# Hybrid decoder layer on one core: the delta rule's triangular inverse in 32-column blocks, and a reordered last expert

## The chip, the cores and the metric

One core of a Trainium2 chip runs the whole program. The metric is device time in microseconds; lower is better. The engines are TensorE (PE; its weight loads are shown as PEld), VectorE (DVE), ScalarE (ACT), GpSimd (POOL) and SyncE (SP, here only a queue of DMAs). TensorE runs at one of two clock levels, 2.4 GHz (shown as 1.0) or 1.2 GHz (shown as 0.5).

## The reference

One decoder layer over 1024 tokens of width 1024, all in float32: an RMS norm; one input projection; a gated MLP mixer (4 heads of 128) beside a gated DeltaNet mixer (4 heads of 128); an output projection with residual; an RMS norm; a router that takes 4 of 32 experts; the experts (width 1024, clamped SwiGLU); a residual; a final RMS norm. What the change touches is the DeltaNet's triangular solve and the end of the layer:

```python
lower = jnp.where(tril_strict, jnp.einsum('bhnid,bhnjd->bhnij', kb, kc) * decay, 0.0)
a_mat = lower + jnp.eye(c, dtype=lower.dtype)
rhs = jnp.concatenate([vc * bc[..., None], kb * jnp.exp(gc)[..., None]], axis=-1)
sol = lax.linalg.triangular_solve(a_mat, rhs, left_side=True, lower=True, unit_diagonal=True)
...
return ((up + 1.0) * (gate * jax.nn.sigmoid(SWIGLU_ALPHA * gate))) @ w_down[e] + b_down[e]
...
return rmsnorm(h, final_norm_g)
```

## The kernel before

Three stages follow each other: projections (to about 361 us), mixers (to about 690 us), experts (to the end). Each engine has its own program, and semaphores tie them; the order of the work is the order in which each engine's program is written.

**Mixers.** The 1024 tokens are 8 chunks of 128, handled as 4 pairs i = 0 to 3; within a pair the two chunks s = 0 and 1 go through each step one behind the other, four heads side by side, so that most tiles are 128 x 512 (four heads of 128 x 128). PSUM has 8 banks; chunk s has banks 4s to 4s+3. For each chunk the kernel needs the inverse T of the unit lower triangular 128 x 128 matrix of each head, and it uses its transpose U.

The inverse is built by doubling (`chunk(i)` on PE and DVE). Level 0 is done elementwise: T starts as the identity minus the 2 x 2 off-diagonal entries (`first_t` on POOL, L891, then two DVE operations, L1310 and L1312), and U as its transpose (`first_u` on POOL, L862 and L864). LT, the masked and scaled product of keys and keys, is made by DVE at L1308. Then for levels l = 1 to 6, for each s: PE multiplies LT by T (`four`, L1036; for l = 5 and 6 only the blocks that count, `lower_blocks`, L1044); DVE masks the product with the level's mask into P (L1321, L1324, L1328); PE multiplies U by P (L1036, L1044); DVE subtracts the result from T (L1338, L1344). From l = 2 on PE also transposes T (L1128) and ACT copies it out of PSUM as the new U (L990). Level 6 is applied to U instead (L1145, L1349). A float32 product leaves two MATMUL records and two LDWEIGHTS records in the trace, a transpose one.

Between the levels stands work of the pair before: two sets of 8 transposes (`h_columns`, L1063, at l = 1 and 3) and the router's logits of both chunks (L1069, at l = 5). After level 6 PE makes W (`four`, L1036), then values, state and outputs. Ahead of level 1 PE makes keys times keys (L1085), keys times queries (L1091), and transposes values (L1104) and keys (L1112). DVE also makes AT (L1316) and ke (L1334) in this stretch. POOL masks the decays E (L845), scales the queries (L850), and writes the token lists by indirect DMA (L883). After the inverse and the state, DVE and ACT already make the decays of the next pair (`start`).

**Last expert.** An expert's `gate_up` on PE (L1787) makes 8 slices m; for each, DVE clamps (`clamps`, L1957 to L1961), ACT applies the sigmoid (L1697), and POOL multiplies twice (`gated`, L1622 and L1625), which frees DVE for slice m + 2. `down_rows` (L1800) takes slice k of hT as soon as it is there. In the last expert the final norm is mixed in: SP has begun to load the 8 tiles of h back (L1559); ACT's `early_squares` takes two tiles' squares (L1702) behind each of the sigmoids m = 4 to 7; DVE takes the means, POOL the roots, DVE scales tiles (L2003), and SP stores them (L1563). The last expert's own 128 rows are treated apart: when its `gated` is over, POOL gathers those rows of h (`hg`, L1656); DVE adds the bias (L2040) and the expert's result (L2030), ACT squares (L1733), and POOL scatters them to the output (L1663) once all tiles are stored.

Of the kernel before, what the change touches and what calls it, by code (L numbers as in the profile page):

```python
# [20 lines left out]
KT, TT = D // P, SEQ // P  # L21
# [22 lines left out]
PARTS, HB = 5, 64  # L44

C_ID, C_TRI, C_ONE, C_M0T, C_LV = 0, 128, 256, 384, 512
C_IOTA = C_LV + LEVELS * 128
# [5 lines left out]
NCST = C_PART + 1  # L53


def program(nc, x, norm_mix_g, w_in, gm_norm_g, gm_ws, gm_bs, dn_conv_w, dn_a_log, dn_dt_bias,
# [6 lines left out]
    with ctx:  # L63
# [14 lines left out]
        m0t = cst[:, C_M0T:C_M0T + 128]  # L78
# [4 lines left out]
        def level(l):  # L83
            return cst[:, C_LV + 128 * l:C_LV + 128 * (l + 1)]
# [29 lines left out]
        AW = 46784  # L114
# [61 lines left out]
        ixf, rkf = [[cut(4) for _ in range(2)] for _ in range(2)]  # L176

# [36 lines left out]
        def heads(ap):  # L214
            return ap.rearrange("p (h c) -> p h c", h=H)

# [623 lines left out]
        def _(pool):  # L840
# [17 lines left out]
            def first_u(i):  # L858

                for s in range(2):  # L860
                    pool.wait_ge(S("LT", s), i + 1)
                    v.tensor_tensor(heads(Um[s]), heads(LT[s]), over_heads(m0t), ALU.mult).then_inc(S("U0a", s), 1)  # L862
                    pool.wait_ge(S("U0a", s), i + 1)
                    v.tensor_tensor(heads(Um[s]), over_heads(ident), heads(Um[s]), ALU.subtract).then_inc(S("U0", s), 1)  # L864
# [21 lines left out]
            def first_t(i):  # L886

                for s in range(2):
                    if i:
                        pool.wait_ge(S("TU", s), 5 * i)  # L890
                    v.tensor_tensor(heads(Tm[s]), over_heads(level(0)), over_cols(sub_all[:, 2 * i + s, :]), ALU.mult  # L891
                                    ).then_inc(S("T0", s), 1)

            first_t(0)
            for s in range(2):
                masked(0, s)
            for i in range(PAIRS):
                first_u(i)
# [7 lines left out]
                if i + 1 < PAIRS:  # L906
                    first_t(i + 1)
                    start(i + 1)
# [20 lines left out]
        def _(act):  # L929
# [40 lines left out]
            def finish(i):  # L970
# [16 lines left out]
                for l in range(2, LEVELS):  # L987
                    for s in range(2):
                        act.wait_ge(S("TU", s), 5 * i + l - 1)
                        a.activation(Um[s], bank(4 * s), ACT.Copy).then_inc(S("Uc", s), 1)  # L990
                    if i and l in (2, 4):
                        hT_copy(i - 1, l // 2 - 1)
                    if i and l in (3, 5):
                        h_norm(i - 1, l // 2 - 1)
                    if i and l == 6:
                        for s in range(2):
                            logits(i - 1, s)
# [31 lines left out]
        def _(pe):  # L1029
# [9 lines left out]
            def lower_blocks(out_bank, left, right, l, name):  # L1039
                b = 1 << l  # L1040
                for h in range(H):
                    for z in range(0, P, 2 * b):
                        lo, hi = slice(h * P + z, h * P + z + b), slice(h * P + z + b, h * P + z + 2 * b)
                        last = t_.matmul(out_bank[z + b:z + 2 * b, lo], left[:, hi], right[:, lo], start=True, stop=True)  # L1044
# [32 lines left out]
            def chunk(i):  # L1077
# [9 lines left out]

                def queries(s):
# [8 lines left out]
                for s in range(2):  # L1097
                    queries(s)
                for s in range(2):
                    b0, c = 4 * s, 2 * i + s  # L1100
                    if i:
                        pe.wait_ge(S("Eb", s), i + 1)
# [12 lines left out]
                for l in range(1, LEVELS):  # L1115
                    for s in range(2):
                        b0 = 4 * s
                        pe.wait_ge(S("Tl", s), 6 * i + l)
                        if l < PARTS:
                            four(bank(b0 + 2), LT[s], Tm[s], S("LTp", s))  # L1120
                        else:
                            lower_blocks(bank(b0 + 2), LT[s], Tm[s], l, S("LTp", s))
                        if l == 2:
# [1007 lines left out]
```

## Time and profile before

| | us |
|---|---|
| median of 3 runs | 2282.27 (2279.67 to 2283.38) |
| profiled execution, device time | 2280.05 |
| its span | 2278.3 |
| PE busy | 2214.6 (97%) |
| DVE, ACT, POOL busy | 747.3, 372.1, 586.4 |

The profile is of one execution; its span is what the engines show and its device time is 1.75 us longer. PE busy counts the time in which at least one matmul record is open, and ends of matmuls are modelled, so it does not tell PE at its peak. Times below are counted from the start of the span.

### The profile page before, as it was taken

Reading aid. Unit: us, or ns where it says so; the run is one execution under the profiler, and the core shown is the slowest. Engines: PE = TensorE matmul, PEld = TensorE weight load, DVE = VectorE, ACT = ScalarE, POOL = GpSimd, SP = SyncE. Lnnn points to the kernel's source line nnn. Section 1 sums busy time; section 2 is a strip of 40 time slices with the busy share of each in tenths; the row PEclk is TensorE's granted clock in tenths of the full one; section 3 lists DMA queues with packets and bytes.
Section 4 is the critical chain, followed back from the end, with each engine's and each line's share of the span. In section 5 each row is a group of like instructions: output and inputs, shape, how many; then the busy total and the mean of one; then the engine's idle time right before and its main releaser. Section 6 shows DMA issues by size and latency. Waiting matters only on the chain.

```text
span 2278.3 us, 45334 instructions
## 1 busy us (share of the span) xinstructions
PE 2214.6 (97%) x18872; PEld 1832.8 (80%) x18873; DVE 747.3 (33%) x1759; ACT 372.1 (16%) x845; POOL 586.4 (26%) x808
## 2 busy tenths in 40 slices
PE   8999998999996999999999999999999999999997
PEld 5665446678765989898898989889898898898975
DVE  2234777454632172222222222222222222213223
ACT  2222653223220101010100101001010010110102
POOL 1133222322423122222222223222232223222312
PEclk9999999999997999999999999999999999999999
DMA  8000113011017788888989799998999979899897
GB/s 266 1 0 19 21 36 154 19 47 47 29 38 252 265 266 279 289 268 275 297 273 319 237 337 296 293 322 284 306 302 293 334 243 336 272 349 351 261 322 285
DMA packets 381977, 505.81 MB, mean 222 GB/s; under 512 B 19248, under 2 KB 295284, under 8 KB 381720
## 3 DMA queue, kind: packets, MB, share of 16 engines
q1 hardware_dynamic: 362632, 459.58, 60.3%
q0 software_dynamic: 19136, 43.29, 7.1%
q8 instruction: 151, 2.47, 0.5%
q14 instruction: 58, 0.48, 0.1%
HBM read 472.19 MB, written 33.05 MB: 222 GB/s over the span
## 4 chain that ended last, share of the span: by engine, by line
PE 73%; SPq 5%; issue 2%; DVE 2%; DMA 1%; POOL 1%; ACT 0%; DVEq 0%; ACTq 0%; POOLq 0%
PE ps L1787 37%; PE ps L1815 12%; PE ps L1800 8%; PE ps L1213 5%; PE ps L1036 3%; SPq L784 3%; PE ps L1765 2%; SPq L1545 1%; PE ps L1774 1%; PE ps L1128 1%; DMA arena<-h_dram,arena 1%; PE ps L1069 1%; SPq L1555 1%; DMA arena<-h_dram 1%; PE ps L1044 0%
## 5 line engine op out<-in xcount | busy, mean ns | idle before, releaser
L1787 PEld LDWEIGHTS ps<-arena 128*64 128x64 f32 (+1 forms) x12544 | 961.6, 152 | 20.0 <-issue 17.7
L1787 PE MATMUL ps<-arena 128*64 128x108 f32 (+29 forms) x12544 | 973.9, 273 | 2.5 <-issue 1.7
L1957 DVE TENSOR_SCALAR arena<-ps,arena 128x108 f32<-128x108 f32 (+29 forms) x256 | 92.3, 361 | 1062.4 <-PE ps L1787 1058.4
L1622 POOL TENSOR_TENSOR arena<-arena 128x108 f32<-128x108 f32 (+29 forms) x256 | 133.1, 520 | 1076.0 <-DVEq L1964 1076.0
L1815 PE MATMUL ps<-arena 128*128 128x224 f32 (+14 forms) x1920 | 273.4, 303 | 0.2 <-POOL arena L1625 0.2
L1697 ACT ACTIVATE arena<-arena 128x108 f32<-128x108 f32 (+29 forms) x256 | 81.5, 318 | 1172.5 <-DVE arena L1957 1172.5
L1815 PEld LDWEIGHTS ps<-arena 128*128 128x128 f32 x1920 | 270.4, 189 | 1.0 <-POOL arena L1625 0.4
L1800 PE MATMUL ps<-arena 128*128 128x512 f32 x544 | 238.6, 596 | 2.7 <-POOL arena L1625 2.7
L1800 PEld LDWEIGHTS ps<-arena 128*128 128x128 f32 x544 | 102.5, 191 | 126.7 <-issue 121.6
L536 PE MATMUL ps<-arena 128*128 128x384 f32 (+1 forms) x512 | 171.5, 494 | 2.1 <-DVE arena L639 2.1
L536 PEld LDWEIGHTS ps<-arena 128*128 128x128 f32 x512 | 97.4, 193 | 68.2 <-issue 2.6
L549 PE MATMUL ps<-arena 128*128 128x512 f32 x336 | 146.3, 593 | 0.8 <-DVE arena L686 0.8
L549 PEld LDWEIGHTS ps<-arena 128*128 128x128 f32 x336 | 63.6, 190 | 80.4 <-issue 78.4
L1625 POOL TENSOR_TENSOR arena<-arena 128x108 f32<-128x108 f32 (+29 forms) x256 | 123.0, 480 | 20.1
L1213 PE MATMUL ps<-arena 128*128 128x512 f32 x256 | 112.9, 595 | 0.8 <-DVE arena L1381 0.8
L232 POOL TENSOR_TENSOR small<-small,cst 128x4 f32<-128x4 f32 (+1 forms) x35 | 27.7, 795 | 332.7 <-DVE small L229 323.2
L1213 PEld LDWEIGHTS ps<-arena 128*128 128x128 f32 x256 | 47.5, 190 | 56.1 <-issue 54.5
L1958 DVE TENSOR_SCALAR arena<-ps,arena 128x108 f32<-128x108 f32 (+29 forms) x256 | 89.9, 351 | 0.0
L1613 POOL DMA_INDIRECT h_dram<-arena x46 | 80.6, 1752 | 30.7 <-issue 15.8
L1036 PE MATMUL ps<-arena 128*128 128x128 f32 x640 | 83.2, 280 | 3.8 <-DVE arena L1321 2.9
L1717 ACT ACTIVATE arena<-ps,arena 128x224 f32<-128x224 f32 (+14 forms) x120 | 47.9, 399 | 231.8 <-PE ps L1815 231.8
L1036 PEld LDWEIGHTS ps<-arena 128*128 128x128 f32 x640 | 76.8, 191 | 5.7 <-issue 3.6
(275 smaller groups left out, 1591.0 us busy)
## 6 DMA issues: line engine op xcount, KB each, us to landing
arena<-in_exp_w_gu SPq DMA_DIRECT2D x256, 1024.0 KB, 10.4
arena<-in_exp_w_down SPq DMA_DIRECT2D x64, 2048.0 KB, 11.6
arena<-in_exp_b_down SPq DMA_DIRECT2D x17, 512.0 KB, 10.1
arena<-in_x SPq DMA_DIRECT2D x16, 512.0 KB, 8.9
arena<-in_w_in SPq DMA_DIRECT2D x8, 1024.0 KB, 9.6
h_dram<-arena SPq DMA_DIRECT2D x16, 512.0 KB, 2.8
arena<-in_w_out SPq DMA_DIRECT2D x1, 4096.0 KB, 14.2
arena<-h_dram SPq DMA_DIRECT2D x8, 512.0 KB, 13.5
```

What stands on the lines that cost most here:

```text
L536: last = t_.matmul(bank(bk)[:, to:to + width], yT[:, k, t * P:(t + 1) * P], wuvz[:, k, c0:c0 + width], start=(k == 0), stop=(k == KT - 1))
L549: last = t_.matmul(to, left[:, k, :], right[:, k, :], start=(k == 0), stop=(k == KH - 1))
L1036: last = t_.matmul(out_bank[:, c], left[:, c], right[:, c], start=start, stop=stop)
L1213: last = t_.matmul(bank(4 * s + 1 + n), mixT[s][:, k, :], wout[:, k, 512 * n:512 * (n + 1)], start=(k == 0), stop=(k == KT - 1))
L1622: v.tensor_tensor(gmn[m % 2][:, 0:n], gmn[m % 2][:, 0:n], umn[m % 2][:, 0:n], ALU.mult).then_inc(S("gum", m % 2), 1)
L1625: v.tensor_tensor(hT[:, m, 0:n], gmn[m % 2][:, 0:n], sg[m % 2][:, 0:n], ALU.mult).then_inc(S("hT"), 1)
L1697: a.activation(sg[m % 2][:, 0:n], gmn[m % 2][:, 0:n], ACT.Sigmoid, scale=ALPHA).then_inc(S("sg", m % 2), 1)
L1787: last = t_.matmul(bank(m % 4)[c0:c1, q * CAP:q * CAP + n], wslot[g][:, k, 256 * q + c + c0:256 * q + c + c1], xT[:, k, 0:n], start=(k == ...
L1800: last = t_.matmul(bank(6 + q), hT[:, k, 0:P], wslot[4 + q][:, k, :], start=(k == 0), stop=(k == KT - 1))
L1815: last = t_.matmul(bank(6 + d % 2)[:, 0:n], wslot[g][:, k, c:c + P], hT[:, k, 0:n], start=(k == 0), stop=(k == KT - 1))
L1957: v.tensor_scalar(gmn[r][:, 0:n], bank(m % 4)[:, 0:n], of[:, m:m + 1], LIMIT, ALU.add, ALU.min).then_inc(S("gmn", r), 1)
L1958: v.tensor_scalar(umn[r][:, 0:n], bank(m % 4)[:, CAP:CAP + n], of[:, 8 + m:9 + m], LIMIT, ALU.add, ALU.min)
```

## The change

- The levels l = 1 to 4 of the inverse stay inside the 32 x 32 blocks on the diagonal. They are held compactly: Tc and Uc are 128 x 128 for a chunk (4 heads of 32 columns; the four blocks of a head lie in the four quarters of the partitions). PE makes the compact keys product itself (`key_blocks`), DVE makes the level 0 T and transposes it blockwise (`v.transpose`).
- `diag_blocks` replaces `four`: 16 products with a weight tile of 32 columns and 32 moving columns each, whose outputs lie in the four quarters of PSUM's partitions. The U side is summed in PSUM: an identity product adds the old U, the second product adds the level's term (the masks are now negative). DVE transposes the result into the new Tc, ACT copies it as Uc. PE's transposes (L1128) go away.
- Level 5 joins 32 blocks to 64 (`join_blocks`, `joined_upper`), with a compact LT copied by ACT (LH) and an expanded U built by DVE; level 6 works as before with a compact T (Th) and copies instead of subtracting.
- LD, the decays masked to the diagonal blocks, is made ahead by POOL (`diag_decays`), which loses `first_u`; DVE multiplies both LD and LT with the keys product. P is still a 128 x 512 tile, written by DVE from a 128 x 128 PSUM tile by a broadcast over the four blocks, for l = 1 to 5.
- Last expert: all 8 sigmoids come first, then ACT squares tiles 2 to 7; DVE squares tiles 0 and 1 itself after the clamps; POOL's two roots come after the gather of `hg`; DVE scales tiles 0 to 3, adds the bias to `hg`, scales tiles 4 to 7, and then does the two halves of the last rows.

```diff
+            def diag_blocks(out_bank, left, right, name=None, start=True, stop=True):
                 for h in range(H):
+                    for z in range(Z):
+                        q = slice(QB * z, QB * (z + 1))
+                        last = t_.matmul(out_bank[q, QB * h:QB * (h + 1)], left(h, z), right[:, QB * h:QB * (h + 1)],
+                                         start=start and h == 0, stop=stop and h == H - 1)
...
+            def joined_upper(out_bank, left, right, name):
+                for h in range(H):
+                    for z, c in ((0, 0), (1, 0), (2, 2)):
...
                 for s in range(2):
+                    if i:
+                        pe.wait_ge(S("Eb", s), i + 1)
+                    key_blocks(s)
...
+                        if l < LEVELS - 2:
+                            diag_blocks(bank(b0 + 2), block_columns(LD[s]), Tc[s], S("LTp", s))
+                        elif l == LEVELS - 2:
+                            pe.wait_ge(S("LH", s), i + 1)
+                            join_blocks(bank(b0 + 2), LH[s], Tc[s], S("LTp", s))
...
+                        if l < LEVELS - 2:
+                            diag_blocks(bank(b0 + 3), block_ident, Uc[s], stop=False)
+                        pe.wait_ge(S("Pl", s), 6 * i + l)
+                        if l < LEVELS - 2:
+                            diag_blocks(bank(b0 + 3), block_columns(Pm[s]), Uc[s], S("TP", s), start=False)
+                        elif l == LEVELS - 2:
+                            joined_upper(bank(b0 + 3), Pm[s], Uc[s], S("TP", s))
...
# DVE, chunk(i)
+                    v.tensor_tensor(Tc[s], Tc[s], bank(4 * s + 3)[:, 0:P], ALU.mult).then_inc(S("Gc_used", s), 1)
...
+                    v.tensor_tensor(blocks(Tc[s]), blocks(Tc[s]), over_heads(ident_b), ALU.add)
...
+                    v.transpose(Uc[s], Tc[s]).then_inc(S("Tl", s), 1)
...
+                    v.tensor_tensor(LD[s], LD[s], bank(4 * s + 2), ALU.mult)
+                    v.tensor_tensor(LT[s], LT[s], bank(4 * s + 2), ALU.mult)
...
+                        if l < LEVELS - 1:
+                            v.tensor_tensor(Pm[s].rearrange("p (h z c) -> p h z c", h=H, z=Z),
+                                            blocks(bank(4 * s + 2)[:, 0:P]).unsqueeze(2).broadcast_to([P, H, Z, QB]),
+                                            blocks(level(l)).unsqueeze(1).broadcast_to([P, H, Z, QB]), ALU.mult).then_inc(S("Pl", s), 1)
...
-                            v.tensor_tensor(Tm[s], Tm[s], bank(b0 + 3), ALU.subtract).then_inc(S("Tl", s), 1)
+                            v.transpose(Tc[s], bank(b0 + 3)[:, 0:P]).then_inc(S("Tl", s), 1)
...
# ACT, last expert
-                sigmoid(r, ROWS[r], early_squares if r == LAST else lambda m: None)
+                sigmoid(r, ROWS[r])
+                if r == LAST:
+                    for t in range(2, TT):
+                        tile_square(t, 0)
...
# DVE, last expert
-            for t in range(2, 4):
+            for t in range(2):
+                dve.wait_ge(S("hc_in", t), 16)
+                v.tensor_tensor_reduce(yt[:, t, :], hc[:, t, :], hc[:, t, :], 1.0, 0.0, ALU.mult, ALU.add, small[:, 32 + t:33 + t])
```

## Rows read from the trace of the kernel before

**Rows 1.** The page: busy time by engine, and the chain that ended last.

```profile
PE 2214.6 (97%) x18872; PEld 1832.8 (80%) x18873; DVE 747.3 (33%) x1759; ACT 372.1 (16%) x845; POOL 586.4 (26%) x808
...
PE 73%; SPq 5%; issue 2%; DVE 2%; DMA 1%; POOL 1%; ACT 0%; DVEq 0%; ACTq 0%; POOLq 0%
```

**Rows 2.** Busy by stretch: length, PE, PEld, DVE, ACT, POOL, clock, DMA, GB/s.

```profile
375.32:389.33 14.01, 14.01 (x122) 13.77 (x122) 8.84 (x14) 3.58 (x6) 1.19 (x1) 1.00 0.56 230
389.33:396.14 6.81, 6.42 (x113) 5.17 (x112) 3.99 (x12) 2.39 (x4) 0.00 (x0) 1.00 0.01 2
438.88:450.14 11.26, 10.42 (x89) 9.98 (x88) 10.59 (x15) 5.38 (x18) 5.71 (x4) 1.00 0.12 49
450.14:464.72 14.58, 14.58 (x130) 14.44 (x129) 8.02 (x14) 6.58 (x11) 1.09 (x2) 1.00 0.09 37
464.72:475.22 10.50, 10.11 (x146) 8.82 (x145) 3.98 (x12) 3.78 (x7) 0.00 (x0) 1.00 0.42 151
...
626.13:638.11 11.98, 11.59 (x146) 10.00 (x145) 3.98 (x12) 3.78 (x7) 0.00 (x0) 0.86 0.38 133
```

**Rows 3.** Timeline, level 2 of pair 2: start, length, engine, line, records, [idle before].

```profile
530.12 1.06 PE L1036 MATMUL ps<-arena 128*128 128x128 f32 x8
...
531.01 0.60 PE L1128 MATMUL ps<-cst,arena 128*128 128x128 f32 x4
531.21 0.69 DVE L1321 TENSOR_TENSOR arena<-ps,cst 128x512 f32<-128x512 f32 x1 [0.65 <-PE ps L1036]
...
532.78 3.00 PE L1036 MATMUL ps<-arena 128*128 128x128 f32 x24
```

**Rows 4.** Timeline, matmuls with weight tiles under 128 columns.

```profile
544.70 0.45 PE L1044 MATMUL ps<-arena 128*32 128x32 f32 x16
...
471.46 0.68 PE L1044 MATMUL ps<-arena 128*64 128x64 f32 x8
...
790.21 7.04 PE L1787 MATMUL ps<-arena 128*64 128x88 f32 x179
```

**Rows 5.** Timeline at the start of pair 2, and DVE by form over its inverse.

```profile
519.79 1.16 PE L1085 MATMUL ps<-arena 128*128 128x128 f32 x8
...
525.37 1.27 DVE L1316 TENSOR_TENSOR arena<-arena,ps 128x512 f32<-128x512 f32 x2
...
L1324 DVE TENSOR_TENSOR arena<-ps,cst 128x128 f32<-128x128 f32 x4 | 1.0, 284 | 0.3 <-PE ps L1044 0.3
```

**Rows 6.** The router's logits of pair 1 (timeline), and the stretch behind them.

```profile
547.75 3.90 PE L1069 MATMUL ps<-rw,arena 128*128 128x32 f32 x32
...
551.20:554.60 3.40, 3.40 (x23) 2.89 (x22) 0.42 (x1) 0.60 (x1) 0.00 (x0) 0.50 0.78 283
```

**Rows 7.** Timeline of the last two experts, and the stores by line.

```profile
2206.49 13.90 PE L1800 MATMUL ps<-arena 128*128 128x512 f32 x32
...
2220.32 27.74 PE L1787 MATMUL ps<-arena 128*64 128x126 f32 x512
...
2245.54 1.06 ACT L1702 ACTIVATE arena<-arena 128x1024 f32<-128x1024 f32 x1 [7.07 <-DMA arena<-h_dram]
...
2248.05 0.31 ACT L1697 ACTIVATE arena<-arena 128x126 f32<-128x126 f32 x1
...
2257.25 9.69 PE L1800 MATMUL ps<-arena 128*128 128x512 f32 x18 [1.98 <-POOL arena L1625]
2257.48 1.97 POOL L1656 DMA_INDIRECT arena<-h_dram,arena  x1 [0.28 <-issue]
...
2260.96 4.87 DVE L2003 SCALAR_TENSOR_TENSOR arena<-arena,small,fin_g 128x1024 f32<-128x1024 f32 x4 [1.17 <-POOL small L232]
...
2267.17 1.28 DVE L2040 SCALAR_TENSOR_TENSOR arena<-arena 128x1024 f32<-128x1024 f32 x1 [1.33 <-DMA arena<-h_dram,arena]
...
2273.84 1.06 POOL L1663 DMA_INDIRECT out<-arena  x1 [1.71 <-DVE arena L2051]
...
out<-arena SPq DMA_DIRECT2D x8, 512.0 KB, 5.1
```

More of the change, by code:

```diff
@@ L884, in lists @@
                                             ids[:, t, j, :], None).then_inc(S("listed"), 16)
[L886 to L894, printed above, removed]
+            for s in range(2):
+                first_T(0, s)
+            for s in range(2):
+                diag_decays(0, s)
             for s in range(2):
                 masked(0, s)
+            for s in range(2):
+                v.memset(LH[s], 0.0)
+                v.memset(Th[s], 0.0)
+            pool.drain()
+            pool.sem_inc(S("zeros"), 1)
             for i in range(PAIRS):
-                first_u(i)
                 if i:
@@ L906, in _ @@
                 if i + 1 < PAIRS:
-                    first_t(i + 1)
+                    for s in range(2):
+                        first_T(i + 1, s)
+                    for s in (1, 0):
+                        diag_decays(i + 1, s)
                     start(i + 1)
@@ L1086, in keys, with key_blocks @@
                     last.then_inc(S("Gk", s), 1)
+                def key_blocks(s):
+                    for h in range(H):
+                        k_ = qkvT[:, 4 + h, cols(2 * i + s)]
+                        for z in range(Z):
+                            q = slice(QB * z, QB * (z + 1))
+                            last = t_.matmul(bank(4 * s + 3)[q, QB * h:QB * (h + 1)], k_[:, q], k_[:, q], start=True, stop=True)
+                    last.then_inc(S("Gc", s), 1)
                 def queries(s):
@@ L1097, in chunk @@
                 for s in range(2):
+                    if i:
+                        pe.wait_ge(S("Eb", s), i + 1)
+                    key_blocks(s)
+                for s in range(2):
                     queries(s)
@@ L1657, in _ @@
                                     ).then_inc(S("hg_in"), 16)
-            tile_roots(1, 0)
+            for q in range(2):
+                tile_roots(q, 0)
             pool.wait_ge(S("l_var"), 1)
@@ L2041, in _ @@
             dve.drain()
+            for t in range(4, TT):
+                tile_scale(t, 0)
             for q in range(2):
                 last_half(q)
+            dve.wait_ge(S("hT"), 8 * NE)
             dve.wait_ge(S("last_h"), 2)
```

207 lines of the change are left out of this document (122 added, 85 removed).

## The prediction

> **What bounds the kernel now.** I read the page first: PE is open 97% of the span and carries 73% of the chain that ended last [rows 1]. Work taken off another engine is then worth nothing, except where PE waits for it. Next the busy times by stretch, to see what the inverse costs [rows 2]. In pair 1 the stretch from the keys product to level 2 is 11.26 us, levels 2 to 4 are 14.58, level 5, the router's logits and level 6 are 10.50: 36.3 together. Pair 0, without the logits, has 14.01 and 6.81 for the last two, and pair 3 11.98 for the last, at a mean clock of 0.86. The four inverses are thus some 145 us, and in levels 2 to 4 PE is open in every moment (14.58 of 14.58): there the time is PE's own work.
>
> The timeline of one level shows its make-up [rows 3]. A `four` is 8 records in 1.06 us; the last record is open 0.28, so PE gives it (1.06 - 0.28) / 7 = 0.112 per record, 0.90 in all. A set of transposes is 4 records, 0.44. A level has four `four` and two sets of transposes: 3.58 + 0.88 = 4.5 us, and from 530.12 to 534.57 (16 records into the run of 24 that begins at 532.78) it took 4.45. DVE's masking (0.69) and subtraction lie beside it.
>
> **The new level, step by step.** Each level from 1 to 4 now issues, per chunk, three `diag_blocks` (LD times T, the identity times U, P times U) of 16 products, 32 records each: 192 records for both chunks instead of 40. So all hangs on the time of one such record, r. No row has four column groups; the nearest have one or two [rows 4]. 16 records with 32-column weights, in two column groups, took 0.45 us: (0.45 - 0.20) / 15 = 17 ns per record, which is 34 ns within a group. 64-column weights with 64 moving columns in one group took (0.68 - 0.22) / 7 = 65 ns. The experts' 64-column weights in two groups, with 88 moving columns, took (7.04 - 0.24) / 178 = 38 ns, less than the 65: two groups run side by side at no visible loss. If four do, r = 34 / 4 = 8.5 ns; if no more than two do, or if the pace of issue is what the 17 shows, r = 17. I take 12: doubling the groups from one to two is shown, from two to four is not, and the result depends little on where r lies below 13, as the next lines show.
>
> With r = 12 a `diag_blocks` is 0.385 us. From the moment that T of chunk 0 is there: first product to 0.385 (its last record closes at 0.57), DVE's masking 0.60 to 1.29 and for chunk 1 to 1.87 (two in 1.27, as L1316 in [rows 5]), meanwhile PE does chunk 1's product and the identity product (to 1.16), then P times U from 1.35 to 1.74, and chunk 1's two to 2.50. DVE's blockwise transpose of a 128 x 128 tile is not in the trace; the nearest row is a 128 x 128 operation from PSUM, 0.284 [rows 5]; bounds 0.2 and 0.69 (a full 512 wide one). It ends at about 2.25, under chunk 1's product, so PE never waits for it. ACT's copy of U is under the next level's first products. A level: 2.5 us. With r = 8.5 DVE and the semaphores bound it, 2.2; with r = 17 PE is full again, 6 x 0.54 = 3.25. `h_columns` adds its 0.90 at level 3, of which a PE with gaps hides a third.
>
> Levels 2 to 4 of a pair: 3 x 2.5 + 0.6 = 8.1 against 14.6, so -6.5 (r = 8.5: -7.3; r = 17: 10.65, -4.0). Pair 0 has no `h_columns`: 7.5 against 14.0, -6.5.
>
> **Start of a pair.** This is where the change gives back. Two `key_blocks` of 32 records each come in PE's order (0.8 us), and DVE gets more to do before level 1 can begin: for both chunks a 128-wide product, addition and transpose (6 x 0.28), two LD products at 0.64 more than before, less the two T products and additions (2 x 0.68, 2 x 1.23 to 1.65) of today. Set out from 519.79 [rows 5]: DVE cannot start before the compact keys are there (1.5), has Tc and Uc at 3.4, LD and LT of both chunks at 6.1, AT (which stands before the level's masks in DVE's queue) at 7.4, then the masks of level 1 to 8.7; PE's last product of level 1 ends near 9.6, `h_columns` near 10.5. Today level 2 begins at 530.12, 10.3 later. So +0.3 (r = 8.5: -0.2; r = 17: +0.9). If POOL's LD were late it would add to this; POOL needs it right after the decays, some 20 us ahead of its use, and it gives up `first_u`. Only in pair 0 is there no such lead, and the clock is low there: +1.
>
> **Levels 5 and 6.** Level 5 has 16 and 24 records per chunk and two full-width masks; PE reaches the logits at 2.1 to 2.3 instead of 3.05: -0.8. The new work of ACT and DVE for it (U expanded, LH, Th) lies under the 3.9 us of logits [rows 6]; in pair 0 it lies bare and takes the gain back. Level 6 loses two sets of transposes and the wait for U's copy: 2.45 against 3.76, -1.3.
>
> **Sum for the mixers** at r = 12: pairs 1 to 3: -6.5 + 0.3 - 0.8 - 1.3 = -8.3 each; pair 0: -6.5 + 1 - 0.9 = -6.4; together -31.3. At r = 8.5 -36, at r = 17 3 x -5.2 - 3.9 = -19.5.
>
> **The clock.** In pair 2 it fell to 1.2 GHz during the logits, whose records move only 32 columns each, and stayed there for the next 3.4 us [rows 6]; pair 3's last stretch has 11.98 where pair 1's has 10.50 at full clock [rows 2], so a fall costs 1.5 us, and two of three pairs pay it. The new levels 1 to 5 also move 32 columns per record, and DVE leaves PE gaps in them. I charge one fall more per pair, 4 us in all (bounds: 0, and the rival below).
>
> **The last expert.** ACT sat idle 7.07 us for the first tile of h, so that the sixth sigmoid came at 2248.05, when PE was at the end of `gate_up` (2220.32 + 27.74) [rows 7]. So `down_rows`, 13.9 us when undisturbed, ended only at 2266.94, and POOL's gather of the last rows, behind `gated`, was issued at 2257.48, landed at 2267.17 and set the end. With the sigmoids first, hT is complete at about 2250.5, PE ends at 2262, and the gather is issued at 2250.5, landing even at 9.7 us by 2260.2. What is late next is DVE: two squares (1.3 each, as L2003) to 2252.5, four scales from 2253.7 to 2258.8, the bias to 2260.1, four scales (4.87) to 2265.2, two halves to 2266.7. Today they cannot end before 2267.17 + 1.28 + 2 x 0.69 = 2269.8; the rest of the chain is the same, unless the last store, 5.1 us to landing from 2265.3, comes last: 2270.4 against today's issue of the scatter at 2273.84. Gain 3 us, bounds 1.5 (stores slower) and 4.
>
> **Forecast.** -31.3 + 4 - 3 = -30. The sum is made against the profiled execution, 2280.05 (span 2278.3), which lies 2.2 below the median shown: 2250 there, 2253 against a median of 2282.3 with 1 us left for what I priced too well. Its own range, r from 8.5 to 14 and the clock's charge from 0 to 8: 2242 to 2259.
>
> **Rivals.**
> - A, two groups' pace: r = 17. For it: the only row with 32-column weights shows it, and each record also needs a weight load. Against: 34 ns within a group fits loads that run beside each other. Time: -19.5 + 3 - 3 = -19.5, 2263.
> - B, a long burst of 96 or 192 small records is issued more slowly than the burst of 16 that the row shows: r = 25, midway between 17 and the 34 of one group by itself. A level is then 192 x 25 = 4.8 us on PE against 4.5, the start +1.9, levels 5 and 6 -1.9: +0.6 per pair, +2 in all, tail -3, clock +2: 2283, no change. Against it: the experts' 179 records run as evenly as short ones [rows 4].
> - C, slower: the clock falls in level 1, as it did in the logits, and stays at 1.2 GHz to level 6, and r doubles from 17 to 34. A level is then 6 x 1.09 = 6.5, three of them and `h_columns` +6, the start +4, level 6 -1.3: +8 to +9 per pair, +33; tail -3: 2312. The place is every pair's levels 1 to 5; it decides from r = 24 on, where the pair is even. For it: [rows 6]. Against: today's level 6 ran cold for 3.4 us only and then came back, though its records are small too.
> - D, the change doesn't reach the end of the tail: the stores' bandwidth, not ACT, sets it. Then only the 3 us go: 2256, inside the forecast.
>
> On B, the Trainium skill (TensorEngine Tiling, section Instruction Overhead) says that each matmul has about 60 cycles of overhead, so that a few moving columns take as long as 60; by that rule the result would be B's. As far as bursts of 16 go, this case's trace disagrees: 17 ns per record, weight load included.
>
> **Chances.** Forecast (with D) 0.60, A 0.23, B 0.07, C 0.07, better than the range 0.03. Faster by over 0.2% (4.6 us, about what can be told from no change) 0.87, within 0.06, slower 0.07. The range that holds 8 in 10 reaches from all groups in parallel to A with a little more clock loss: 2242 to 2267.
>
> **What would show it.** The level's spacing of L1321's successor: 2.5 us (2.2 and 3.25 the bounds, 4.8 for B, 6.5 for C). Records of a `diag_blocks`: 32 in 0.27 to 0.54 us plus the last one's length. The clock in levels 1 to 5: 1.0 in most of it. Level 2 of pair 2 begins 10.5 us after the second keys product. DVE's transpose near 0.28; if it were 0.69, a level is 2.9. At the end: PE done near 2262 less the mixers' gain, no idle in it. The prediction is wrong if r is over 17, if the clock falls inside the levels for more than a third of them, or if a level is bound by an ACT or DVE operation priced here as hidden.

## The result: slower by 0.8%, and the profile after

The changed kernel took 2299.95 us (median of 4 runs, 2296.42 to 2303.46) against 2281.68 for the kernel before (4 runs, 2279.67 to 2283.38): a ratio of 1.0078, 95% interval 1.0066 to 1.009. The forecast was 2253, its range 2242 to 2267. The direction was wrong. One execution further down stands apart, 4624.37 us for the 100-record version at its second measurement; why is not known, and it is in no time and no ratio given here.

The page of the kernel after, lines that answer to [rows 1], with the queue that carries instructions:

```profile
PE 2197.6 (95%) x21592; PEld 1815.1 (79%) x21593; DVE 738.9 (32%) x1771; ACT 369.5 (16%) x881; POOL 569.8 (25%) x804
...
q8 instruction: 172, 2.82, 0.5%
...
PE 75%; issue 4%; DVE 3%; POOL 1%; DVEq 1%; DMA 1%; another core or an unknown queue 0%; POOLq 0%; ACT 0%; SPq 0%; ACTq 0%
```

PE is open 17 us less than before, in a span that is 23.3 longer (2301.6 against 2278.3): the work went down as meant, and time in which PE does nothing took its place. "Issue", time in which an engine waits for nothing that the profile shows, went from 2% to 4% of the chain. The mean granted clock went from 0.988 to 0.969. The queue q8 moved 151 packets before and 172 now: 21 more, for 5520 more instructions on the page (50854 against 45334), which is one packet for 263.

Where the 23.3 lie: the program reaches the first keys product 1.7 later (in the profiles of the later runs this point lies between 362.1 and 364.3 us, so that is spread between executions); from there to W, the four pairs together took 165.4 instead of 145.5 (+19.9); behind W, pairs 1 and 2 take 1.4 longer each (0.78 of it one more wait for DVE ahead of the products in L1138); from the last W to the experts nothing changed; first product of the experts to the end of the span, 1.3 less, the tail in it. The busy rows by stretch, pair 0 from the last products of level 1 to the first joins of level 5, then pair 1 in three stretches as in [rows 2], and the last stretch of pair 3:

```profile
376.45:400.00 23.55, 11.66 (x702) 10.54 (x704) 8.33 (x18) 2.63 (x10) 0.00 (x0) 0.55 0.38 153
448.90:460.06 11.16, 9.74 (x313) 8.93 (x311) 8.73 (x19) 6.65 (x23) 0.00 (x0) 1.00 0.13 51
460.06:475.59 15.53, 9.60 (x585) 8.73 (x584) 5.63 (x14) 4.61 (x11) 1.08 (x2) 0.67 0.10 38
475.59:490.69 15.10, 12.80 (x164) 12.28 (x149) 4.78 (x10) 4.33 (x13) 0.00 (x0) 0.58 0.31 106
648.74:662.72 13.98, 12.97 (x161) 12.35 (x149) 4.81 (x10) 4.07 (x12) 0.00 (x0) 0.51 0.32 115
```

The start of pair 1 takes 11.16 against 11.26. Levels 2 to 4 take 15.53 against 14.58 (8.1 were forecast), though PE is open only 9.60 of it and DVE 5.63: no engine's work fills this stretch. Level 5, logits and level 6 take 15.10 against 10.50, at a clock of 0.58.

The timeline of pair 2 shows why, PE's rows of levels 2 to 4 and of the logits (start, length, records, [idle before <- what ended it]):

```profile
544.80 0.46 PE L1084 MATMUL ps<-arena 128*32 128x32 f32 x32 [1.20 <-DVE arena L1415]
...
550.04 0.35 PE L1084 MATMUL ps<-arena 128*32 128x32 f32 x18 [0.72 <-issue]
...
553.77 0.48 PE L1084 MATMUL ps<-arena 128*32 128x32 f32 x18 [2.07 <-issue]
554.01 0.67 PE L1084 MATMUL ps<-arena,cst 128*32 128x32 f32 x32
...
557.78 0.48 PE L1084 MATMUL ps<-arena 128*32 128x32 f32 x18 [2.08 <-issue]
558.20 1.97 PE L1127 MATMUL ps<-cst,arena 128*128 128x128 f32 x8
...
566.05 6.42 PE L1133 MATMUL ps<-rw,arena 128*128 128x32 f32 x32
```

The record itself is as fast as the best bound: 32 records in 0.46, the last of them open 0.20, so (0.46 - 0.20) / 31 = 8.4 ns. But after 128 records (550.04 to 553.77, then to 557.78) PE stops, with every input there, and goes on 2.1 us later. 256 records took 7.74 us, 30 ns each. From 554 on the row of 32 records takes 0.67 instead of 0.46: the clock has fallen to 1.2 GHz. Read in steps of 1 us, the granted clock of pair 2 is 0.50 from 554 to 563, 1.00 from 564 to 566, and 0.50 again from 567 to 577, through the rest of the logits (6.42 against 3.90 in [rows 6]) and level 6. Pairs 1 and 3 also fall twice: in the levels (464 to 474, 638 to 645) and from level 5 on (478 to 491, 649 to 662).

### The profile page after: what moved, and what is told of

It reads as the page before. It is cut to its first block, busy times and chain, and to the rows that moved or that the text cites. A ratio compares the mean times of both kernels' runs of the same rounds, so it can differ in the third digit from the quotient of the medians.

```text
span 2301.6 us, 50854 instructions
## 1 busy us (share of the span) xinstructions
PE 2197.6 (95%) x21592; PEld 1815.1 (79%) x21593; DVE 738.9 (32%) x1771; ACT 369.5 (16%) x881; POOL 569.8 (25%) x804
## 3 DMA queue, kind: packets, MB, share of 16 engines
q8 instruction: 172, 2.82, 0.5%
## 4 chain that ended last, share of the span: by engine, by line
PE 75%; issue 4%; DVE 3%; POOL 1%; DVEq 1%; DMA 1%; another core or an unknown queue 0%; POOLq 0%; ACT 0%; SPq 0%; ACTq 0%
PE ps L1878 39%; PE ps L1906 12%; PE ps L1891 10%; PE ps L1297 4%; PE ps L1856 2%; PE ps L1084 2%; PE ps L1865 1%; PE ps L1133 1%; PE ps L1077 1%; PE ps L1149 0%; PE ps L1127 0%; POOL arena L1717 0%; PE ps L1255 0%; POOL arena L1714 0%; DMA arena<-h_dram,arena 0%
## 5 line engine op out<-in xcount | busy, mean ns | idle before, releaser
L1906 PEld LDWEIGHTS ps<-arena 128*128 128x128 f32 x1920 | 270.4, 189 | 1.0 <-POOL arena L1717 0.4
L1891 PEld LDWEIGHTS ps<-arena 128*128 128x128 f32 x544 | 102.0, 190 | 122.1 <-issue 121.4
L551 PEld LDWEIGHTS ps<-arena 128*128 128x128 f32 x512 | 97.9, 194 | 68.7 <-issue 3.5
L1717 POOL TENSOR_TENSOR arena<-arena 128x108 f32<-128x108 f32 (+29 forms) x256 | 123.0, 481 | 20.1
L564 PEld LDWEIGHTS ps<-arena 128*128 128x128 f32 x336 | 63.6, 190 | 80.4 <-issue 78.4
L1297 PEld LDWEIGHTS ps<-arena 128*128 128x128 f32 x256 | 47.5, 190 | 56.1 <-issue 54.5
L2052 DVE TENSOR_SCALAR arena<-arena 128x108 f32<-128x108 f32 (+29 forms) x256 | 61.0, 238 | 31.6 <-issue 0.9
L734 DVE SCALAR_TENSOR_TENSOR arena<-arena,vT 128x512 f32<-128x512 f32 x72 | 66.5, 923 | 6.3 <-issue 0.9
```

Of the source, the lines that this page charges most:

```text
L551: last = t_.matmul(bank(bk)[:, to:to + width], yT[:, k, t * P:(t + 1) * P], wuvz[:, k, c0:c0 + width], start=(k == 0), stop=(k == KT - 1))
L564: last = t_.matmul(to, left[:, k, :], right[:, k, :], start=(k == 0), stop=(k == KH - 1))
L1297: last = t_.matmul(bank(4 * s + 1 + n), mixT[s][:, k, :], wout[:, k, 512 * n:512 * (n + 1)], start=(k == 0), stop=(k == KT - 1))
L1717: v.tensor_tensor(hT[:, m, 0:n], gmn[m % 2][:, 0:n], sg[m % 2][:, 0:n], ALU.mult).then_inc(S("hT"), 1)
L1891: last = t_.matmul(bank(6 + q), hT[:, k, 0:P], wslot[4 + q][:, k, :], start=(k == 0), stop=(k == KT - 1))
L1906: last = t_.matmul(bank(6 + d % 2)[:, 0:n], wslot[g][:, k, c:c + P], hT[:, k, 0:n], start=(k == 0), stop=(k == KT - 1))
```

## Experiments

All ran against the kernel before, on the same chip as the others of their group. Three theories stood against each other. **S**: instructions reach PE at a limited pace, and 192 records a level ask for more. **K**: the fallen clock is what costs. **W**: waits between PE, DVE and ACT bound the new levels. S and K can hold together.

### The tail alone

The kernel before with only the second half of the change: the last expert's sigmoids ahead of the norm's squares.

```
- gated(r, ROWS[r], (lambda m: scatter_main(r - 1, m)) if r < LAST else (lambda m: tile_roots(0, 0) if m == 5 else None))
+ gated(r, ROWS[r], lambda m: scatter_main(r - 1, m))
...
- sigmoid(r, ROWS[r], early_squares if r == LAST else lambda m: None)
+ sigmoid(r, ROWS[r])
+ if r == LAST:
+     for t in range(2, TT):
+         tile_square(t, 0)
```

> The kernel before with the new order of the last expert alone (squares after the sigmoids, two of them on DVE, roots after the gather). In the two profiles the stretch from the first record of the last down_rows to the end of the span is 30.3 us before (2247.99 to 2278.3) and 27.95 after (2273.65 to 2301.6). So 2.3 us faster than before, ratio 0.9990. If the order does nothing by itself, and the 2.3 us come from another state of the DMAs after the slower mixers: 0 us.

Measured: 2279.63 (11 runs), ratio 0.9994, interval 0.9985 to 1.0003. That is 1.9 us less, which the timing can't tell from nothing. The profiled executions say more: from the first record of the last `down_rows` to the end of the span it takes 28.0 here, as in the changed kernel (28.0), against 30.3 before. So the 2.3 us belong to the new order and not to the slower mixers ahead of it. The loss is all in the inverse.

### One identity product in place of sixteen

```
- diag_blocks(bank(b0 + 3), block_ident, Uc[s], stop=False)
+ t_.matmul(bank(b0 + 3)[:, 0:P], ident, Uc[s], start=True, stop=False)
```

The identity product of a chunk and level is now one matmul (2 records in place of 32), with the same result: 132 records a level in place of 192.

> The changed kernel, but the identity product of a level is one 128 x 128 product per chunk (2 records) in place of 16 small ones (32 records): 132 records per level instead of 192, the PE time of them about the same (0.22 us against 0.27 at full clock). Theory S (supply): PE gets its instructions at a pace of 128 records (with their weight loads) per 3.6 to 4.0 us once a stock is used up, so 60 records fewer are 1.8 us less per level, 16 levels: 25 to 29 us faster than the changed kernel, near 2273 us, and the gaps that the trace puts down to issue shrink by a third or more. Theory K (clock): the granted clock is the cause and the gaps are only its effect: PE's work is unchanged, so the time stays within 5 us of the changed kernel (2300). Theory W (the chain over DVE, ACT and semaphores bounds a level): unchanged too, 2300.

Measured: 2268.69 (6 runs, 2262.5 to 2274.28), ratio 0.9945, interval 0.993 to 0.996: 31 us less than the change, and faster than the kernel before. S had asked for 25 to 29 less; K and W had asked for no change, and both failed. PE's groups in the mixers, first of the kernel after, then of this one (records | busy, mean ns | idle before, and what ended it):

```profile
L1084 PE MATMUL ps<-arena 128*32 128x32 f32 x2048 | 34.7, 218 | 20.3 <-issue 12.3 <-DVE arena L1415 5.3 <-DVEq L1405 2.1
...
L1084 PE MATMUL ps<-arena,cst 128*32 128x32 f32 x1024 | 20.7, 219 | 17.3 <-issue 17.3
```

```profile
L1084 PE MATMUL ps<-arena 128*32 128x32 f32 x2048 | 31.6, 208 | 13.8 <-issue 5.5 <-DVE arena L1415 4.3 <-DVEq L1405 2.6
L1216 PE MATMUL ps<-arena,cst 128*128 128x128 f32 x64 | 17.7, 360 | 1.2 <-issue 1.2
```

In these groups the idle time that ends with "issue" went from 12.3 + 17.3 = 29.6 to 5.5 + 1.2 = 6.7. The waits for DVE hardly moved, 7.4 to 6.9: W explains none of the difference. Over the four pairs PE's idle time went from 42.9 to 19.4, and its open time from 122.5 to 114.1 at a mean clock of 0.981 over the span instead of 0.969. So some 24 of the 32 us that the pairs got shorter are supply; the other 8 are less open time, at a higher clock.

### The pace of supply by itself

Bursts of independent small products before the mixers, in the kernel before (ident times the table of constants, its output not used; one run, 2452.08 us, for their durations alone), and one more in the expert stage. Sixteen wide products ahead of each burst let instructions pile up.

```
+ wide(16); burst(256, 32, 32, 4)     # weights 32 wide, 32 columns moved, 4 column groups
+ wide(16); burst(256, 64, 64, 2)
+ wide(16); burst(256, 32, 128, 4)
+ wide(16); burst(256, 32, 32, 1)
```

> The kernel before with products added that nothing waits for and nobody reads, at the head of the mixers (after the load of w_out) and once behind the sixth expert: bursts of 512 records between stretches of 16 wide products (128 x 512) that keep the clock up. Burst 1: 32-column weights, 32 moving columns, four column groups. Burst 2: 64, 64, two groups. Burst 3: 32-column weights, 128 moving, four groups. Burst 4: as 1 but all in one group. In the expert stage burst 1 again, under weight traffic. S: burst 1 runs at 8.5 ns per record for one stock and then in portions of 128 records per 3.6 to 4.0 us, 12 to 15 us in all with gaps of 2 us or more, at full clock and with no wait in the program; bursts 2 and 3 (27 to 32 ns per record by width) lie at the edge, 14 to 17 us, gaps under 1 us; burst 4 (34 ns) has none, 17.4 us. If gaps belong to waits or to the low clock and not to supply: burst 1 takes 512 x 8.5 ns = 4.4 us without a gap. Under traffic: S leaves open whether the portions come later; 3.6 us if the traffic does not matter.

PE's rows of the first burst (512 records, between two wide products), and what the DMAs moved from 390 to 404 us, in 40 slices of 0.35 us:

```profile
391.83 1.48 PE L1225 MATMUL ps<-cst 128*32 128x32 f32 x150
395.33 1.30 PE L1225 MATMUL ps<-cst 128*32 128x32 f32 x128 [2.02 <-issue]
398.80 1.94 PE L1225 MATMUL ps<-cst 128*32 128x32 f32 x128 [2.16 <-issue]
402.26 1.70 PE L1225 MATMUL ps<-cst 128*32 128x32 f32 x106 [1.52 <-issue]
...
GB/s 0 0 0 0 0 0 0 0 47 0 0 0 0 0 0 0 0 0 47 0 0 0 0 0 0 0 0 0 47 0 0 0 0 0 0 0 0 0 47 0
...
q8 instruction: 4, 0.07, 1.8%
```

This is S with nothing else in it: no data is waited for, and at full speed PE takes 150 records in 1.48 us, then gets portions of exactly 128 every 3.47 us. The whole burst takes 12.1 us, where S had asked for 12 to 15. In its second gap, at 397.3, the granted clock falls from 1.00 to 0.50; the portions behind it run cold (1.94 and 1.70) and come no later, so the pace does not hang on that clock.

A record stands for two instructions, the weight load and the product, so a portion is 256 instructions, 27 ns per record. The instruction queue moved four packets in 14 us here, and nothing else was moved; on the page it has packets of 16.4 KB (2.82 MB / 172), which is 64 bytes for each of 256 instructions. The trace also shows what the 3.47 us are made of. The packets start at 392.89, 396.37 and 399.88, each 2.4 us ahead of a portion, and each 1.0 to 1.1 us after the portion before it began (the first, after the burst began). So no packet starts before PE has begun on the portion before. That is the order in the trace; what imposes it is not shown.

The other bursts had no such gaps, and their records are slower than that: 29.6 ns (64-wide weights), 28 (128 columns moved), 32 (one column group). In the expert stage, under weight traffic, the stock was 162 records and the portions came 3.47 us apart as well, after a first gap of 3.26.

### Weights of 64 columns: no gaps, but the clock

```
-                    for z in range(Z):
-                        q = slice(QB * z, QB * (z + 1))
+                    for z in range(2):
+                        q = slice(HB * z, HB * (z + 1))
```

(on top of the single identity product; the blocks off the diagonal are zero, so two 64-wide products do the work of four, and a level has 68 records.)

> As the one before, and the block products use weight tiles of 64 columns (two 32-blocks at once, the masks keep them apart), so 8 products instead of 16: 68 records per level. S: 68 records are supplied in about 2.0 us, so supply no longer binds; PE needs 64 x 0.033 + 0.45 = 2.6 us per level at full clock, level near 2.8 us, against 4.5 of before and about 4.3 to 5 of the changed kernel: 15 to 25 us faster than before, 2257 to 2267 us; no gaps put down to issue in levels 1 to 4. K: PE's share rises, the clock may hold, but if the clock was the cause the gaps stay. W: 2300, as the chain over DVE and ACT is the same.

Measured: 2286.5 (12 runs, spread from 2266.19 to 2291.56), ratio 1.0001, interval 0.9981 to 1.0021. No PE row in the levels ends its idle time with "issue" any more, so S alone would have made this the best version (2257 to 2267); two of the 12 runs come near it. Keys product to W of pairs 1 and 2, the same instructions in the same execution:

```profile
442.21:485.30 43.09, 41.80 (x546) 37.96 (x544) 19.40 (x42) 15.70 (x46) 1.08 (x2) 0.63 0.18 63
530.87:562.11 31.24, 29.76 (x546) 26.92 (x544) 19.14 (x42) 15.71 (x46) 1.09 (x2) 0.95 0.25 87
```

At a mean clock of 0.95 the pair takes 31.2, at 0.63 it takes 43.1. The clock alone is worth 12 us a pair when the work is PE's own, and the runs follow it: the two at 2266 and 2268 us have a mean clock over the span of 0.98, the eight from 2284 on 0.969 to 0.972. In the first of these two pairs the clock falls at 453 and stays at 0.50 until 487, though PE is open in every moment from 452 to 473. So it can fall and stay low without gaps for want of instructions.

### Filling PE with idle products

Two idle products per chunk and level 1 to 4, into columns of U's bank that nobody reads, in the changed kernel, in the version with 64-wide weights, and one product in the version with a single identity product:

```
+                        if l < LEVELS - 2:
+                            for _ in range(2):
+                                t_.matmul(bank(b0 + 3)[:, P:4 * P], ident, cst[:, 0:3 * P],
+                                          start=True, stop=True)
```

> The changed kernel with two idle wide products of 384 columns (ident by the table of constants, into columns 128 to 511 of U's bank, which nobody reads) per chunk at each of levels 1 to 4, behind the wait for Uc and ahead of the identity products. Nothing else changes: the 192 small records of a level stay. Price of one, from L1220 of the probe (0.44 us for 512 columns at full clock): 0.33 us, so 1.3 us of PE a level, 5.2 us a pair, 21 us in all if none of it lies in time in which PE stands idle. Theory S+K (the small records arrive at 128 per 3.5 to 4.0 us, and the clock falls because PE does little in that time): the filling lies in the idle 2 us per 128 records and costs 0 to 7 us; the granted clock stays up through the levels of more pairs, and the 10 to 12 us that a pair at 1.2 GHz loses come back for one to three pairs: 2265 to 2292 us, mean clock at 0.975 or above. Theory S alone (the supply is all of it, the clock an effect that costs nothing of its own): 2300 to 2307 us. Theory W (the chain over DVE and ACT bounds the levels): filling ahead of the identity products delays it: 2305 to 2321 us.

Measured for the changed kernel with filling: 2301.18 (5 runs), ratio 1.0086, interval 1.0073 to 1.01, mean clock 0.984. By its letter the expectation of S alone was met and that of S and K missed. But the price in it was wrong. The filling's rows in level 2 of pair 1, and the windows of that pair in the three stretches:

```profile
462.43 1.56 PE L1217 MATMUL ps<-cst 128*128 128x384 f32 x4
463.92 0.46 PE L1084 MATMUL ps<-arena,cst 128*32 128x32 f32 x32
...
464.61 1.56 PE L1217 MATMUL ps<-cst 128*128 128x384 f32 x4
```

```profile
448.83:461.74 12.91, 12.69 (x322) 10.28 (x320) 9.01 (x21) 6.92 (x24) 0.49 (x1) 1.00 0.12 44
461.74:478.35 16.61, 16.44 (x609) 10.86 (x609) 5.44 (x11) 4.71 (x10) 0.60 (x2) 1.00 0.10 37
478.35:487.87 9.52, 8.94 (x162) 8.47 (x148) 4.75 (x10) 4.07 (x12) 0.00 (x0) 0.82 0.48 167
```

A product is two records. The row shows 4 records, two products, in 1.49 (462.43 to 463.92): 0.37 a record, 0.75 a product, and I had priced a product at the time of one record. The filling is thus 64 products x 0.75 = 48 us of PE work, not 21, and it cost 1 to 2 us against the changed kernel (2301.18 and 2299.95; ratios 1.0086 and 1.0078). The four pairs took 162.7 instead of 165.4 with the 48 in them, so some 50 us of room were found. About 33 of it was idle time of PE (42.9 to 10.3 in the pairs; the "issue" groups fell from 29.6 to 3.9). The other 18 came back in PE's own work (122.5 before, 152.4 - 48 = 104 now), at a clock that is 1.00 in the levels where it was 0.67. So the third stretch of pair 1 takes 9.52 where the changed kernel had 15.10, and the levels are full of PE work that is not wanted. Of the four pairs' 163 only 115 are work that is wanted, and waits.

> The kernel with weights of 64 columns (68 records a level, no idle time for want of instructions, but pairs that run at 1.2 GHz) with the same two idle products of 384 columns per chunk and level. It adds up to 21 us of PE work and takes none away. Theory K (what this version loses is the clock alone, 12 us for each pair that falls): the clock is granted through the levels, mean 0.98 or above, and the time is 2262 to 2284 us, below the 2286.5 of the version without the filling although it does more. If the clock is not what costs: 2287 to 2308 us, mean clock as before.

Measured for 64-wide weights with filling: 2296.71 (5 runs), ratio 1.0076, interval 1.0062 to 1.009, mean clock 0.988: the clock held in all four pairs (0.92 to 1.00), and of 48 us added 10 show in the medians, 17 in the ratios (the version without filling spreads over 25). By its time K was missed again, for the same wrong price; its clock came. The other 31 to 38 came back from the clock. PE's waits gave next to nothing: in the two profiles its idle time in the pairs is 7.1 without the filling and 5.4 with it.

> The version with one identity product (132 records a level, 2268.7 us, mean clock 0.979 to 0.983) with one idle product of 384 columns per chunk and level (0.33 us each, 10.5 us in all if none lies in idle time). Theory S+K: about half lies in the idle time that the supply leaves (13.8 us behind L1084 in that version), and the stretches that still fell to 1.2 GHz fall less: 2255 to 2270 us. Without an effect of the clock: 2271 to 2279 us.

Measured for the single identity product with filling: 2273.01 (8 runs), ratio 0.9967, interval 0.9957 to 0.9978, clock 0.985: 24 us added and 4 to 5 shown (2268.69, ratio 0.9945, without). The time lies where the expectation put a clock without effect (2271 to 2279), again by the wrong price: it takes a give-back of some 19 us to get there. Filling holds the clock but never pays for itself over all four pairs.

### 100 records a level

The single identity product, and L times T with 64-wide weights, P times U left at 32:

```
+            def half_blocks(out_bank, left, right, name):
+                for h in range(H):
+                    for z in range(2):
+                        q = slice(HB * z, HB * (z + 1))
+                        last = t_.matmul(out_bank[q, QB * h:QB * (h + 1)],
+                                         left[:, P * h + HB * z:P * h + HB * (z + 1)], ...)
...
- diag_blocks(bank(b0 + 2), block_columns(LD[s]), Tc[s], S("LTp", s))
+ half_blocks(bank(b0 + 2), LD[s], Tc[s], S("LTp", s))
```

> The version with one identity product, and the product of L by T with weights of 64 columns: 100 records a level in place of 132, the same results. Theory S: the supply asks 2.7 us a level in place of 3.6, so the idle time for want of instructions in the levels (13.8 us behind L1084) goes and 6 to 12 us come back: 2257 to 2263 us. Theory K (fewer and longer records let the clock fall, as with 64 columns throughout): pairs fall to 1.2 GHz and the time is 2268 to 2290 us, mean clock under 0.978.

Measured: 2262.36 (5 runs, 2261.92 to 2267.04), ratio 0.9927, interval 0.9913 to 0.994; the same kernel on another chip 2265.33 (5 runs), ratio 0.9928, interval 0.9915 to 0.9941. S's time came (2257 to 2263) on the first chip, and K's (2268 to 2290) on neither. Pair 1 in the three stretches:

```profile
440.50:451.81 11.31, 10.42 (x222) 9.32 (x220) 8.88 (x21) 6.69 (x24) 0.00 (x0) 1.00 0.13 49
451.81:460.81 9.00, 9.00 (x310) 7.78 (x310) 5.49 (x12) 4.80 (x11) 1.08 (x2) 1.00 0.17 62
460.81:471.91 11.10, 10.52 (x164) 10.07 (x150) 4.73 (x10) 4.13 (x13) 0.00 (x0) 0.69 0.43 145
```

Levels 2 to 4 take 9.00 against 14.58 before and 15.53 in the change, and PE is open in every moment. Pair 2 still has one wait for instructions, 0.66 of its 9.90. The last stretch still falls to 1.2 GHz in the logits, with no gap for want of instructions ahead of it, as in pairs 2 and 3 of the kernel before [rows 6].

### Filling in pair 0 alone

Pair 0 of that version took 35.3 us, more than before (33.5): it stands idle 3.5 us for want of instructions and then runs cold. So one idle product per chunk and level, in pair 0 only.

> The version with 100 records a level (2262.4 us) with one idle product of 384 columns per chunk and level 1 to 4, in pair 0 alone (8 products, 0.37 us each by their row in the filled version, 3.0 us). In that pair PE stood idle 3.50 us for want of instructions (378.6 to 382.5) and the clock was 1.2 GHz from there to the first W (397.8); keys product to W took 35.3 us, against 30.5 to 31.4 in the other pairs. Theory S+K: the filling lies in the 3.5 us, the clock stays, and the later levels and the joins run at full pace: pair 0 takes 31 to 34 us, 2258 to 2262 us in all. If the clock in pair 0 costs nothing of its own, or falls all the same: 2262 to 2266 us.

> The version with 100 records a level once more, unchanged, on the same chip as the version that fills pair 0, for their comparison: 2260 to 2265 us, faster than the kernel before by 16 to 21 us; supply of instructions and clock as before it.

Measured: 2260.9 (5 runs, 2257.2 to 2263.6) with the filling and 2265.33 (5 runs, 2260.96 to 2266.06) without, ratios to before 0.9913 (0.99 to 0.9926) and 0.9928 (0.9915 to 0.9941). The first time lies in the range given for S and K, the second 0.3 over its own. The intervals overlap, and the profiled executions place the difference elsewhere than I said. Keys product to W, with the filling and without:

```profile
362.09:397.62 35.53, 30.61 (x640) 25.09 (x640) 21.16 (x42) 9.74 (x36) 10.14 (x12) 0.88 0.55 218
```

```profile
363.83:397.71 33.88, 30.90 (x624) 26.91 (x624) 21.76 (x42) 9.76 (x36) 10.13 (x12) 0.65 0.58 229
```

The clock rose from 0.65 to 0.88 and pair 0 gained nothing: 35.5 against 33.9 there (35.3 in the earlier execution of the same version). The price was again that of a record; the 8 products are 6.0 us of PE work, not 3.0. The last two pairs were 1.6 and 0.8 shorter instead. The expectation for pair 0 failed, and whether the filling gains anything over the whole run stays open.

## Why the prediction was wrong, step by step

**The step that failed** is the first of the level: "With r = 12 a `diag_blocks` is 0.385 us ... A level: 2.5 us". It made the time of a level from the time of a record, and took the record's time from short bursts. The record was right (8.4 ns, the lower bound, all four column groups at once), and by it the level was to be 2.2. What sets the level is how many records the supply brings: 128 per 3.5 to 4.0 us, once 4.6 and once 6.2, so 192 records take 5.2 to 6 or more where no stock is left. Levels 2 to 4 of pair 1 measured 15.53, `h_columns` in it, against 8.1 forecast. No term of the sum had such a limit, and the only place where it stood was rival B, which has its mechanism (a long burst issued more slowly) at 25 ns a record, close to the 27 of the probe. Its 4.8 us a level was nearly right. I gave it 0.07 because "the experts' 179 records run as evenly as short ones". Those records take 38 ns each, slower than the supply, so they could not show its limit; and of PE's groups between 360 us and the end of the kernel before, only the experts' `gate_up` ends idle time with "issue", 1.7 us in all. A short burst does not show the limit either, since 150 to 162 records were in stock when the bare bursts began. The evidence that I held against B was blind to B.

The Trainium skill (TensorE: Matmul & The Clock Gate, section "Wait — 56ns, not 53.3ns?") says that the start-to-start time of small matmuls never drops below about 25 ns. The rows disagree as to the matmul, 8.4 ns with its weight load. An estimate by that rule gives a level 192 x 25 ns = 4.8 us, near what was measured, for another reason.

**The clock.** I charged 4 us for it. It is rival C's mechanism that came in on top of B's, in two spells per pair: 1.2 GHz in the middle of the levels, and again from level 5 through the logits and level 6. C had doubled the record's time for its price; but in the levels the record is not what binds (13.9 ns at 1.2 GHz, still less than the supply's 27), and cold portions come no further apart for it (3.46 to 3.74 us in pair 0, all at 0.50). The main price is behind the levels: logits 6.42 in pair 2 and 7.04 in pairs 1 and 3, against 3.90 and 3.76, +2.5 and +3.3, and level 5 and the joins. That is the 4.6 us by which the third stretch of pair 1 is longer than before, where -2.1 was forecast (levels 5 and 6).

What lets the clock go stays open. In the levels it fell inside a gap of 2 to 3 us, as in the bare burst, and with the filling in the same place it did not; but with 64-wide weights it fell and stayed low while PE was open throughout, and the kernel before and the 100-record version lose it in the logits. So the gaps are not its only occasion. C's sign and time (2312) came closer than my own, for a sum of two smaller effects.

**Start of a pair: right.** 11.16 for pair 1 and 12.00 for pair 2 against 11.26 and 11.28; +0.3 was forecast. DVE's blockwise transpose took 0.30 to 0.32 from PSUM and two from SBUF 0.50, against 0.28 taken. In pair 0, where I charged 1, the start takes 13.53 (364.34 to 377.87) against 12.70, +0.8; but levels 2 to 4 take 21.06 (to 398.93) where 7.5 was forecast and 14.01 measured before, since its instructions come more slowly: 133 records in 9.34 us.

```profile
377.87:387.21 9.34, 2.42 (x133) 2.11 (x133) 2.34 (x5) 0.81 (x3) 0.00 (x0) 0.56 0.76 314
```

That stretch has 314 GB/s of transfers beside it where levels 2 to 4 of pair 1 have 38. The trace shows where the time goes. PE's portions at 381.01 and 387.21 start 2.5 and 2.4 us after their packets of instructions, as in the bare burst; but the second packet starts only 3.8 us after the portion at 381.01, where 1.1 is usual, and 1.2 MB of loads move in between. In pair 1 the one packet that comes late (2.1 us, portions 4.6 apart) has 0.5 MB of loads ahead of it. That the loads delay the fetching of instructions fits both, but no run took them away, and the expert stage's portions came 3.47 apart under its own traffic. It stays open.

**Levels hidden under PE: right in kind.** From level 2 to level 4 PE waits for DVE 0.2 to 0.4 us at a time, and for ACT not at all; in the 100-record version PE is open 9.00 of 9.00 in pair 1.

**The tail: right, a little small.** `down_rows` to the end of the span takes 28.0 against 30.3, so 2.3 in the profile, and 1.9, not clear of nothing, in the timed run; 3 was forecast, with bounds of 1.5 and 4. The order is as foretold, the gather first and the scales next; these are the rows that answer to [rows 7]:

```profile
2273.65 14.00 PE L1891 MATMUL ps<-arena 128*128 128x512 f32 x32
...
2277.02 1.80 POOL L1748 DMA_INDIRECT arena<-h_dram,arena  x1 [0.15 <-issue]
...
2291.77 1.40 DVE L2115 SCALAR_TENSOR_TENSOR arena<-ps,arena 128x512 f32<-128x512 f32 x2
...
2297.16 1.07 POOL L1756 DMA_INDIRECT out<-arena  x1 [1.71 <-DVE arena L2142]
```

PE runs `down_rows` without a break; the gather goes out 3.4 us after its start, where I had 2.5, behind a gate's product on POOL (L1717) that took 1.31 beside DVE's first square and 0.45 in the slices before, and DVE's last halves end 19.5 after it instead of 18.7.

**Where the forecast's gain is.** It can be had: the 100-record version makes the mixers' pairs 1 to 3 shorter by 4.9, 7.1 and 7.3 (forecast 8.3 each) and pair 0 longer by 1.8 (forecast 6.4 shorter), and is the faster kernel by 0.7%. That is 17.6 of the 31.3. Of the 13.7 that are missing, pair 0 has 8.2 and pair 1, with its cold logits, 3.4.

## What to carry to other kernels

Count instructions per stretch, not only their duration: in these runs PE got 256 of them (128 weight loads with their products) each 3.5 us, and splitting a product into blocks pays only while the new stretch stays under that pace. One full-width product that wastes three quarters of its multiplications (2 records, 0.42 us) was better than sixteen exact ones (32 records, 0.27 us of PE, but 0.86 us of supply). A burst that fits into the stock, or whose records are slower than the supply, says nothing about it; and where PE starts to stand idle, look for the clock in the work behind it, which can pay too. Count a filling or any other product by its records: a float32 product had two, and I had priced one.

## What the runs showed of the hardware that I had not expected

- Records of 32 x 32 blocks in four column groups follow each other every 8.4 ns at 2.4 GHz, weight loads included, and every 13.9 ns at 1.2 GHz; in one group 32 ns.
- The supply is in steps: nothing for mostly 1.2 to 2.4 us, then 128 records at full pace. In levels with 192 records the steps stood 3.5 to 4.0 us apart, once 4.6 and once 6.2, in the bare burst 3.47. Each step starts 2.2 to 2.6 us after a packet of 16.4 KB on the instruction queue.
- The same program ran between 2266 and 2292 us (64-wide weights), in step with its mean clock (0.982 to 0.969); one pair costs 12 us more cold than warm.
